# Reordered small products in a hybrid decoder layer: level scores inside a weight unit, the first chunk's values and products ahead of a weight split, carried states first in the sample heads, and spin products ahead of FFN1

## What is computed

```python
x = x + 0.5 * swiglu(rmsnorm(x), w_gate, w_up, w_down)      # FFN1, 1024 -> 2816 -> 1024
z = rmsnorm(x) @ w_in                                       # one projection for both mixers
# mLSTM, 4 heads, qk 128, v 128: C_t = f C_{t-1} + i k_t v_t^T, h_t = q_t C_t / max(|q_t n_t|, e^-m_t)
# GLA, 4 heads, k 64, v 128:     S_t = diag(alpha_t) S_{t-1} + k_t^T v_t, o_t = q_t S_t
y = concat(sigmoid(mo) * head_rmsnorm(h_mlstm), silu(gg) * head_rmsnorm(h_gla))
x = x + y @ w_out
x = x + cross_attention(rmsnorm(x), mem_k, mem_v)           # 4 heads over 256 memory tokens
x = x + 0.5 * swiglu(rmsnorm(x), ...)                       # FFN2
# outputs: final rmsnorm of both groups, memory K/V of the prompt, and all new states
```

## Time and profile before

| what | value |
|---|---|
| median of 3 runs (range) | 1360.73 us (1359.83 to 1365.76) |
| the profiled execution | 1365.62 us |
| its span from the first to the last instruction | 1363.8 us |
| mean granted TensorE clock over it | 0.987 |
| busy: PE, DVE, ACT, POOL | 1332.1, 665.6, 429.4, 41.7 us |
| DMA over the span | 138.31 MB, 101 GB/s |

### The profile page before, as it was taken

One profiled execution on the slowest core, in us unless ns is written; L12 is line 12 of the kernel. 1 busy time (PEld: TensorE's weight loads), 2 busy tenths in 40 slices (PEclk: granted clock), 3 DMA queues, 4 the chain that ended last, 5 costly groups with the idle time before them and its releaser, 6 DMA issues.

```text
span 1363.8 us, 25703 instructions
## 1 busy us (share of the span) xinstructions
PE 1332.1 (98%) x10995; PEld 1294.7 (95%) x10995; DVE 665.6 (49%) x903; ACT 429.4 (31%) x644; POOL 41.7 (3%) x64
## 2 busy tenths in 40 slices
PE   7999999999999999998899999999999999999997
PEld 7999999999999999998798898889999999999997
DVE  4554455433333366667666534535454454443332
ACT  6222222222222143245533623324322222222221
POOL 1000000000000000002111000100000000000000
PEclk8999999999999899999899999999999999999998
DMA  6323323323333223224035773533323323323221
GB/s 196 94 80 89 92 81 88 88 74 95 87 74 93 78 79 78 79 78 125 13 115 164 225 238 124 187 139 93 93 79 91 92 80 89 92 74 94 87 70 66
DMA packets 208136, 138.31 MB, mean 101 GB/s; under 512 B 6550, under 2 KB 196224, under 8 KB 208068
## 3 DMA queue, kind: packets, MB, share of 16 engines
q1 hardware_dynamic: 200240, 109.88, 28.0%
q0 software_dynamic: 7664, 27.27, 5.8%
q10 hardware_dynamic: 164, 0.16, 0.0%
HBM read 129.41 MB, written 7.88 MB: 101 GB/s over the span
## 4 chain that ended last, share of the span: by engine, by line
PE 49%; DVE 1%; ACT 0%; issue 0%; ACTq 0%
PE ps L1688 47%; PE ps L2124 1%; PE ps L2228 0%; ACT prob L871 0%; PE ps L2153 0%; DVE xmx L1561 0%; PE ps L2074 0%; DVE kT L1578 0%; PE ps L2102 0%; ACT kT L882 0%; DVE y_raw L1399 0%; DVE prob L1570 0%; DVE q_pad L1643 0%; DVE yf_s L1679 0%; DVE acc L976 0%
## 5 line engine op out<-in xcount | busy, mean ns | idle before, releaser
L1688 PE MATMUL ps<-xn_hi,w_hi 128*128 128x272 f32 x2144 | 449.5, 291 | 2.9 <-ACT xn_hi L573 2.9
L1688 PE MATMUL ps<-xn_hi,w_lo 128*128 128x272 f32 x2144 | 446.3, 289 | 0.0
L1688 PE MATMUL ps<-xn_lo,w_hi 128*128 128x272 f32 x2144 | 445.0, 288 | 0.0
L551 ACT ACTIVATE w_hi<-raw 128x1024 fp32r<-128x1024 f32 x206 | 217.9, 1058 | 650.8 <-PE ps L1688 650.8
L965 DVE TENSOR_TENSOR w_lo<-raw,w_hi 128x1024 fp32r<-128x1024 f32 x206 | 252.4, 1225 | 200.8 <-ACT w_hi L551 199.8
L1688 PEld LDWEIGHTS ps<-xn_hi,w_hi 128*128 128x128 f32 x2144 | 338.5, 190 | 4.2 <-DVE w_lo L965 3.1
L1688 PEld LDWEIGHTS ps<-xn_hi,w_lo 128*128 128x128 f32 x2144 | 339.7, 190 | 0.0
L1688 PEld LDWEIGHTS ps<-xn_lo,w_hi 128*128 128x128 f32 x2144 | 337.9, 190 | 0.0
L1688 PE MATMUL ps<-h_hi,w_hi 128*128 128x272 f32 x704 | 146.0, 289 | 0.0
L1688 PE MATMUL ps<-h_hi,w_lo 128*128 128x272 f32 x704 | 145.5, 288 | 0.0
L1688 PE MATMUL ps<-h_lo,w_hi 128*128 128x272 f32 x704 | 145.1, 287 | 0.0
(11 more groups left out here) (345 smaller groups left out, 1087.6 us busy)
## 6 DMA issues: line engine op xcount, KB each, us to landing
raw<-in_ffn_w_gate SPq DMA_DIRECT2D x44, 512.0 KB, 3.8
raw<-in_ffn_w_up SPq DMA_DIRECT2D x44, 512.0 KB, 3.8
raw<-in_w_in SPq DMA_DIRECT2D x29, 512.0 KB, 3.8
raw<-in_ffn_w_down SPq DMA_DIRECT2D x32, 448.0 KB, 3.7
raw<-in_ffn_w_down SPq DMA_DIRECT2D x16, 512.0 KB, 4.0
kv<-in_cache_mem_k POOLq DMA_DIRECT2D x6, 1024.0 KB, 7.1
kv<-in_cache_mem_v POOLq DMA_DIRECT2D x6, 1024.0 KB, 6.9
raw<-in_w_out SPq DMA_DIRECT2D x8, 512.0 KB, 3.9
```

Of the source, the lines that this page charges most:

```text
L551: act.activation(w_hi[u0 % 2][:, :], raw[u0 % 4][:, :], ACT.Copy).then_inc(sem("hi_done"), 1)
L1688: return pe.matmul(out, lhsT, rhs, start=start, stop=stop)
```

## The change

Five things are moved or added, and no arithmetic on the data changes.

1. **Spins.** `spin(n, bank)` issues n products of the identity with itself into a PSUM bank whose content isn't needed. Six run as soon as the constants are there, ahead of the transposes of x; ten run after the last transposes, ahead of the first unit, once VectorE has read bank 1.
2. **Level scores.** `level_scores` of level n is issued after the third slice (j == 2) of the unit behind `S_SCORES[n]`, no longer between the two units.
3. **First chunk.** ScalarE makes the split of unit U_OUT + 1 after the value and key copies of chunk 0 (before: ahead of them); VectorE makes `chunk_products(0)` ahead of its half of that split.
4. **Chunks.** On ScalarE the values' copies stand ahead of the keys' in every chunk. In `outputs(c)` heads 0 and 1 wait for the first gate of the chunk before, heads 2 and 3 for the second; before, all waited for the second.
5. **Sample heads.** The 32 products with the carried states come first and open the sums; the waits for the sample weights and the products with the values follow, and the denominators come last.

```diff
@@ -719,7 +719,8 @@
             for k in range(NZ):
                 if k + 1 == NZ:
                     weights_exp(0)
-                split(U_IN + k + 2)
+                else:
+                    split(U_IN + k + 2)
                 if k == S_DECAY:
 
                     act.wait_ge(sem("y_decay"), 1)
@@ -817,15 +818,16 @@
                 act.wait_ge(sem("cols_made"), 2)
                 act.activation(kw_s, ps[:, 6, 0:DK], ACT.Copy, scale=scol[:, 3:4]).then_inc(sem("kw_done"), 1)
 
+            value_tokens(0)
             key_tokens(0)
-            value_tokens(0)
+            split(U_OUT + 1)
             for c in range(NC):
                 chunk_squares(c)
                 chunk_scales(c)
                 if c + 1 < NC:
                     weights_exp(c + 1)
+                    value_tokens(c + 1)
                     key_tokens(c + 1)
-                    value_tokens(c + 1)
                 else:
                     sample_copies()
                 chunk_hi(c)
@@ -1457,8 +1459,8 @@
 
             dve.memset(v1_tok[:, :, DV:DV + 1], 1.0).then_inc(sem("tok_set"), 1)
             chunk_weights(0)
+            chunk_products(0)
             split(U_OUT + 1)
-            chunk_products(0)
             for c in range(NC):
                 chunk_dens(c)
                 state_mlstm(c)
@@ -1688,7 +1690,13 @@
                 return pe.matmul(out, lhsT, rhs, start=start, stop=stop)
 
 
+            def spin(n, bank):
+
+                for k in range(n):
+                    mm(ps[:, bank, 0:128], ident, ident)
+
             pe.wait_ge(sem("const_in"), 16)
+            spin(6, 7)
             for c in range(NC):
                 if c == 3:
                     pe.wait_ge(sem("x_act"), 1)
@@ -1703,6 +1711,8 @@
                     ins = pe.transpose(ps[:, 2 * c + d // 4, 128 * (d % 4):128 * (d % 4) + 128],
                                        xp_nat[:, c, d * 128:d * 128 + 128], ident)
                 ins.then_inc(sem("xT_mm"), 1)
+            pe.wait_ge(sem("x_dve"), 1)
+            spin(10, 1)
 
             def norm(g, buf):
 
@@ -1846,11 +1856,12 @@
             for k in range(2, NZ):
                 pe.wait_ge(lo_done, U_IN + k + 1)
                 pe.wait_ge(evac, B_IN + k - (3 if k < Z_GV else 1))
-                unit(U_IN + k, B_IN + k if k < Z_GV else k % 2, xn_hi, xn_lo, 0, 8, True, True)
+                for j in range(ND):
+                    unit(U_IN + k, B_IN + k if k < Z_GV else k % 2, xn_hi, xn_lo, 0, 8, True, True, j)
+                    if j == 2 and k - 1 in S_SCORES:
+                        level_scores(S_SCORES.index(k - 1))
                 if k == S_DECAY - 1:
                     decay_product()
-                if k in S_SCORES:
-                    level_scores(S_SCORES.index(k))
                 if k == S_ROWS + 1:
                     pe.wait_ge(sem("rows_exp"), 3)
                     pe.wait_ge(sem("levels_done"), 1)
@@ -1912,9 +1923,9 @@
                 tt = slice(c * L, (c + 1) * L)
                 pe.wait_ge(sem("p_done"), c + 1)
                 pe.wait_ge(sem("v_done"), c + 1)
-                if c:
-                    pe.wait_ge(sem("y_gated"), 2 * c)
                 for h in range(H):
+                    if c and h % 2 == 0:
+                        pe.wait_ge(sem("y_gated"), 2 * c - 1 + h // 2)
                     dst = sums(0)[:, h // 2, h % 2, :]
                     ins = mm(dst, pw[:, h, :], v1_tok[:, h, :], True, c == 0)
                     if c:
@@ -1973,20 +1984,20 @@
 
             def sample_heads():
 
-                pe.wait_ge(sem("p_done"), NC + 1)
-                pe.wait_ge(sem("v_done"), NC + 1)
                 pe.wait_ge(sem("gs_done"), NC)
-                pe.wait_ge(sem("qn_done"), 1)
-                mm(ps[:, 5, DV:DV + 1], p_heads, ones[:, 0:1], True, False)
-                mm(ps[:, 5, DV:DV + 1], q_in[:, 1, :], ones[:, 0:1], False, True)
-                for h in range(H):
-                    mm(ps[NS * h:NS * h + NS, 5, 0:DV], p_heads[:, NS * h:NS * h + NS], v_s[:, 0:DV], True, False)
                 pe.wait_ge(sem("rows_filled"), 2)
                 pe.wait_ge(sem("state_in"), 16 * H)
                 for b in range(B):
                     for h in range(H):
-                        ins = mm(ps[NS * h:NS * h + NS, 5, 0:DV], q_row[:, h, NS * b:NS * b + NS], ring[:, h, b, :],
-                                 False, b == B - 1)
+                        mm(ps[NS * h:NS * h + NS, 5, 0:DV], q_row[:, h, NS * b:NS * b + NS], ring[:, h, b, :],
+                           b == 0, False)
+                pe.wait_ge(sem("p_done"), NC + 1)
+                pe.wait_ge(sem("v_done"), NC + 1)
+                pe.wait_ge(sem("qn_done"), 1)
+                for h in range(H):
+                    mm(ps[NS * h:NS * h + NS, 5, 0:DV], p_heads[:, NS * h:NS * h + NS], v_s[:, 0:DV], False, True)
+                mm(ps[:, 5, DV:DV + 1], p_heads, ones[:, 0:1], True, False)
+                ins = mm(ps[:, 5, DV:DV + 1], q_in[:, 1, :], ones[:, 0:1], False, True)
                 ins.then_inc(sem("heads_mm"), 1)
                 pe.wait_ge(sem("gv_done"), NC + 1)
                 pe.wait_ge(sem("cn_done"), NC)
```

## The result

The changed kernel takes 1355.3 us (median of 7 runs, 1352.57 to 1356.86) where the kernel before, run beside it, takes 1362.34 (7 runs, 1359.83 to 1365.76): 7.0 us less by the medians. The ratio on record is 0.9941, 95% interval 0.9927 to 0.9954; that is 0.59%, or 8.0 us (6.3 to 9.9). A later set of runs of the same kernel gave 1353.46 against 1362.95, 9.5 us by the medians, ratio 0.9931 (0.9916 to 0.9945), 9.4 us.

The account below looks back on a forecast made before the run. TensorE, busy 1332 of 1363.8 us, was taken as the bound, leaving only its idle time and half-clock stretches to win. Terms of 1.5 + 2.4 + 0.9 + 1.6 + 2.9 = 9.3 us became 8.0 for the median: 1352.7, range 1349.5 to 1358.

Parts of the forecast that it names:

- a wait for lv_qk of over 0.4 us: Sign at the level scores: no such wait was to remain on TensorE after the change.
- Start: Ahead of FFN1: the second spin keeps the first unit at full clock, 1.5 us won; the first spin set at 0.
- Level scores: Scores inside the next unit: both waits for lv_qk, 2.6 us, go except 0.2, so 2.4 us won.
- First chunk: Chunk 0: early products shorten the work before the squares, though the low half delays the denominators; 0.9 us won.
- Chunks 1 to 3: First two heads wait for the first gated half only; 0.64 us for two chunks, half for the middle, 1.6 us.
- Sample heads: Ring products fill the 1.9 us wait, and a third of 2.8 us of clock, 1.0, returns; 2.9 us together.
- The conversion to the median: Whole kernel: the median lies 4.9 us below the profile, so 1.3 of 3.4 us of clock can't be won.
- Nothing given back in the heads: VectorE's chain ends at 680.2, the output projection's first half-unit at about 683, so no wait appears there.
- The rival that the moved waits come back: Chunk 0, unit 15's weight, hidden gates and slow sample heads leave 4.8 us for the median, 1355.9; chance 0.21.
- Slow spins: Rival at the start: the spins run at 1.2 GHz, giving 1355.7 us; chance 0.05.
- a stage held at 1.2 GHz: Rival: new idle time ahead of the first back transposes holds the chunk stage slow, giving 1368 us; chance 0.02.
- idle time ahead of the work: Chunk stage and sample heads: TensorE's idle time may lower its clock; without it the heads gain up to 2.8 us.

Follow-up runs that it names:

- no_second_spin: The changed kernel without spin(10), the spin ahead of the first FFN1 unit; 1359.41 us, ratio 0.9966 to the kernel before.
- no_first_spin: The changed kernel without spin(6), the spin ahead of the x transposes; 1356.39 us, ratio 0.9943 to the kernel before.
- level_alone: The kernel before with only the level scores moved inside the next unit; 1361.38 us, ratio 0.9980.
- old_heads: The changed kernel with the sample heads in their old order; 1358.25 us, ratio 0.9961 to the kernel before.
- heads_alone: The kernel before with only the new order of the sample heads; 1359.24 us, ratio 0.9979.
- split_later: The changed kernel with ScalarE's half of the split behind chunk 0's scales and VectorE's behind its gates; 1351.09 us, ratio 0.9906 to the kernel before.
- after_again: The changed kernel itself, run once more; 1353.46 us, ratio 0.9931 to the kernel before.
- fill_before_back: The changed kernel with nine more dummy products on TensorE ahead of chunk 0's back transposes; 1356.18 us, ratio 0.9946 to the kernel before.
- late_stores: split_later with GpSimd's eight state stores moved from ahead of the sample heads to behind the state updates; 1350.55 us, ratio 0.9921 to the kernel before.
- after: The changed kernel in its first set of runs, with all five parts against the kernel before; median 1355.3 us, ratio 0.9941, profiled execution 1352.57 us.

## Why the prediction was right

The numbers of the stages, from the traces: means over the profiles that lack the part and those that have it (their count in brackets; profiles in which another edit touches the stage are left out, and in the last row `no_second_spin`, whose 5.32 us fall into it; with it the mean is 7.81). The waits for lv_qk are those of the earlier trace rows and of the profile after.

| stage | predicted | without the part | with it | won |
|---|---|---|---|---|
| start, `norm` at | 1.5 | 27.47 (4 profiles) | 25.63 (6) | 1.8 |
| waits for lv_qk | 2.4 | 2.6 | 0.57 | 2.0 |
| last unit of w_in to back(0) | 0.9 | 14.36 (3) | 13.44 (7) | 0.9 |
| back(0) to back(3) | 1.6 | 37.66 (3) | 37.03 (7) | 0.6 |
| back(3) to the output projection | 2.9 | 11.27 (4) | 7.31 (8) | 4.0 |
| sum | 9.3 | | | 9.3 |

That the two sums agree is luck in part: chunks 1 to 3 gave 1.0 us less than predicted and the sample heads 1.1 more. One sign named ahead was missed, a wait for lv_qk of over 0.4 us.

- **Start: right, one term of it wrong.** The unit runs at full clock and waits for the sixth `xn_lo`, 0.59 us, as said. But `spin(6)`, set at 0, seems worth something: in the first profile the transposes end 1.05 us earlier than before (12.26 and 13.31), and 2.15 us are gained, near the upper bound of 2.2. Without it the second spin began at 1.2 GHz in `no_first_spin`, and nothing was won at the start. The gain varies: `level_alone`, with no spin, came to `norm` at 26.15, as early as `old_heads` with both (26.14), since its clock was up from 9.8 us on, where the other starts without a first spin had it from 11.3 to 16.9.
- **Level scores: right.** 0.57 us stayed where 0.2 was predicted; `level_alone` shows that nothing comes back behind them.
- **First chunk: right in mechanism and size.** The low half does hold the denominators (0.2 us later, predicted 0.3), the gain comes from the products being done early, and it exists where TensorE ran slow: with the old order the stage took 14.63 and 15.43 us at a fallen clock but 13.01 in `heads_alone`, 0.4 less than the new order's 13.44, which seven profiles show within 0.02 us, whatever the clock. `split_later` shows what the change left there: 2.1 us to the back transposes, and 3.4 to 4.8 us of time by the ratios.
- **Chunks 1 to 3: mechanism right, the term mis-sized.** The wait of 1.4 us is 0.82 where it shows, ended by the first gate. But the mean is 0.6 us, not 1.6: four of the seven profiles took 35.6 to 36.8 us, and three took 38.1, with the clock at 0.50 for about 7 us of the stage. I had counted on that in one chunk only, with half of its gain. Among profiles with one stretch of 3.4 us at 0.50 in the stage, the old gates took 37.72 and 37.85 us and the new ones 36.22, 36.22 and 36.78: 1.4 us less, near the predicted size.
- **Sample heads: mechanism right, the term mis-sized.** The wait is gone and the clock gives more than a third: of the 2.8 us that I allowed for it, 2.1 come on average, 3.2 in the first profile (5.0 in all, above the upper bound of 4.7), 1.3 in `heads_alone`. Ring products alone give 1.0; the 32 GLA products behind them took 1.92 us in all nine profiles with the new order and 2.35 to 2.71 in the four with the old.
- **The conversion to the median.** The profile's 13.1 us is more than the change: before, 6.8 us of the decay ran at 1.2 GHz, which costs up to 3.4 us, after none, and the change alters nothing there; behind the start of the output projection the profile after took 2.1 us longer than the one before. The median lost 7.0 and 9.5 us; the forecast of 8.0 lies between. That falls of the clock set the runs apart was an inference, and the runs bear it out: of 55 runs of the kernel before beside the experiments, the 14 with a mean granted clock of 0.987 took 1365.2 us on average and the 10 with 0.991 took 1360.8.
- **Nothing given back in the heads: nearly.** In the first profile the output projection up to its `norm` took 0.5 us more (63.76, 63.22 before), 0.29 of it the wait for `y_lo`; in `after_again` it took 63.20.

The rival that the moved waits come back has the low half right, and the rest not. Its 4.8 us lie below both measured gains; that its 1355.9 is nearer to the measured 1355.3 than the forecast's 1352.7 comes mostly from the 1.6 us by which the later runs of the kernel before were slower. Slow spins and a stage held at 1.2 GHz did not come. The reason that I gave for the clock, idle time ahead of the work, is the step that failed. It holds at the start (`no_second_spin`) and for the fall that the first profile after shows behind 2.32 us of idle time, at 626.3. But 14 of the 18 falls in chunks 0 to 2 came with TensorE busy, right behind products over 4 rows, one of them in the kernel before; and in `heads_alone` the ring products were slow behind the same 0.56 us of idle time, ahead of back(3), behind which they were fast in the change. What idle time goes with is how long the clock stayed down. In `after_again` the stretch at 1.2 GHz behind `weights(1)`, with 1.86 us of idle time ahead of back(0) in it, lasted 6.8 us (the line below shows most of it); in `split_later`, with no idle time there, it was 3.4 us. From the chunks to the heads, all 8 of the longer stretches have idle time in them (0.7 to 2.2 us), the 21 short ones next to none (0.24 us at most).

```profile
622.00:628.70 6.70, 4.84 (x24) 0.50 0.75 199
```

The Trainium skill (Perfetto Trace Analysis, Matmul Optimizations) ties the matmul engine's power to its utilization and asks for matmuls issued back to back; `fill_before_back` issued them so, and the clock fell. The Trainium skill (TensorE: Matmul & The Clock Gate, Part 4: PE-mode transpose) has it that transposes don't bring the full clock; of that the runs show this: in four of five starts that have no first spin the last eight transposes took 1.09 us, at full clock, with nothing but transposes before them, and in the fifth 1.97.

## What to carry to other kernels

A split that gives way to one chain must be put behind every chain that its engines serve next: ahead of the denominators it cost most of what it gave, and moved behind the scales and gates it brought the back transposes forward by 2.1 us more. Products whose inputs are ready early (here 64 with carried states) belong into the wait for the late ones, where they pay at either clock. Where a stage's clock changes from one execution to the next, take a term from several profiles: one alone showed 5.0 us for a part that gives 4.0 on average, and 13.1 us for a change that gives 7.0 to 9.5.

## What the runs showed of the hardware

- Products over 4 of 128 rows kept TensorE busy but did not hold 2.4 GHz: the clock fell right behind 14 of 39 groups of 16 with no idle time, and behind the 20 thin passes at the start. They don't bring the fall every time: `late_stores` has the same groups and ran through the stage at 1.00. What decides between the two stays open.
- Around the state stores of chunk 3 and the load behind them, engines stood without a cause in the program: VectorE's gate came 1.93 us after its transposes in the change, 0.49 in `fill_before_back`, TensorE stood 5.32 us in `no_second_spin`, while in the other profiles with the new order the gate follows within 0.12. By the trace's DMA records single packets of that load took up to 4.2 us in the change (median 0.16) and an instruction fetch of 16 KB 3.0 us; in `late_stores`, with the stores elsewhere, none of the load's packets took over 1.5 us, and packets of up to 4.6 us came with the stores, at 729 us. That run alone does not show the stores to be the cause: with the stores in their old place, but the old order of the heads, the load's packets took 1.15 us at most in all four profiles. Over the 12 profiles with the stores in their old place it goes by how soon the load is issued behind the last of them: 3.0 us behind it (`after` and `no_second_spin`, the two that lost 1.9 us or more) its slowest packet took 3.6 to 4.2 us, 4.3 to 4.4 us behind it 2.0 to 2.5, 5.3 us behind it 1.6, and 7.7 to 8.5 us behind it 0.8 to 1.15. So the faster heads bring the load closer to the stores. Why an engine then halts in some executions and not in others stays open.
